# Output projection in four 512-column blocks, and two modulation vectors as TensorE column tiles

## The reference

```python
for i in range(DEPTH):
    mod_lat = silu(c) @ ada_w[i] + ada_b[i]                 # six vectors of 2048
    sh1, sc1, g1, sh2, sc2, g2 = split(mod_lat, 6)
    h_lat = rms_norm(x, norm_mix_g[i]) * (1 + sc1) + sh1
    if i == 0:                                              # 16 heads of 128, 4 key/value heads
        q_l, k_l, v_l = project_qkv(h_lat, ...)             # and rotary on q, k
        k_c, v_c = project_kv(h_ctx, ...)
        o_lat = latent_attention(q_l, k_l, v_l, k_c, v_c) @ attn_w_o
    else:
        o_lat = fourier_mix(h_lat, fourier_w_o)
    x = x + g1 * o_lat
    x = x + g2 * (relu((rms_norm(x, norm_mlp_g[i]) * (1 + sc2) + sh2) @ w1[i]) ** 2 @ w2[i])
return rms_norm(x, final_norm_g)
```

## Time and profile before

| | us |
|---|---|
| median of three runs | 2138.22 (2131.68 to 2138.55) |
| the profiled execution | 2128.54 |
| its span in the trace | 2126.7 |
| TensorE busy | 2018.2 (95%) |
| VectorE busy | 1375.5 (65%) |
| ScalarE busy | 975.3 (46%) |
| mean granted TensorE clock | 0.979 of full |
| mean DMA rate | 253 GB/s |

### The profile page before, as it was taken

How to read it: one execution, slowest core, us unless ns; L and a number is a source line. 1 busy time by engine, 2 the same in 40 slices (tenths; PEclk the granted TensorE clock), 3 DMA queues, 4 the chain that set the end, 5 groups by cost and what they waited for, 6 DMA issues and landing times.

```text
span 2126.7 us, 25114 instructions
## 1 busy us (share of the span) xinstructions
PE 2018.2 (95%) x10348; PEld 1648.6 (78%) x10348; DVE 1375.5 (65%) x1355; ACT 975.3 (46%) x1263; POOL 109.0 (5%) x196
## 2 busy tenths in 40 slices
PE   4999979888999999999999999989999999999997
PEld 3677746656888878788888888878888887888886
DVE  2466879935877868677657866876666545555455
ACT  4433555424445445444444444354554554444443
POOL 1111000100000000000000000000000000000000
PEclk8999999998999999999999999989999999999999
DMA  9798427786998979688759826957777555555653
GB/s 369 280 341 318 168 98 256 260 313 237 335 332 287 358 273 352 241 316 310 268 196 353 349 81 235 377 184 254 246 248 250 188 176 178 198 195 188 213 196 119
DMA packets 140682, 538.89 MB, mean 253 GB/s; under 512 B 8436, under 2 KB 9620, under 8 KB 101012
## 3 DMA queue, kind: packets, MB, share of 16 engines
q1 hardware_dynamic: 106576, 329.73, 44.1%
q0 software_dynamic: 31744, 201.34, 25.8%
q10 hardware_dynamic: 2248, 6.21, 0.8%
HBM read 535.15 MB, written 2.10 MB: 253 GB/s over the span
## 4 chain that ended last, share of the span: by engine, by line
PE 85%; DVE 8%; DMA 3%; ACT 2%; issue 2%; POOL 0%; DVEq 0%; SPq 0%; ACTq 0%; POOLq 0%
PE ps L1515 22%; PE ps L1471 12%; PE ps L1475 12%; PE ps L1474 12%; PE ps L1517 11%; PE ps L1319 4%; PE ps L1320 3%; PE ps L1321 3%; DVE sum_wo L862 1%; DVE ada_sum L862 1%; PE ps L1360 1%; DMA ada_raw<-in_ada_w 1%; DMA c_rows<-in_ctx 1%; DMA spare<-in_ada_w 1%; PE ps L1376 1%
## 5 line engine op out<-in xcount | busy, mean ns | idle before, releaser
L835 DVE TENSOR_TENSOR w_lo<-raw,w_hi 128x1024 fp32r<-128x1024 f32 x624 | 760.1, 1223 | 590.3 <-ACT w_hi L460 590.2
L460 ACT ACTIVATE w_hi<-raw 128x1024 fp32r<-128x1024 f32 x624 | 658.1, 1059 | 905.4 <-PE ps L1475 426.8
L1515 PE MATMUL ps<-hh,w_hi 128*128 128x512 f32 x2048 | 720.0, 397 | 4.0 <-issue 2.6
L1517 PE MATMUL ps<-hh,w_lo 128*128 128x256 f32 x2048 | 571.7, 279 | 0.0
L1515 PEld LDWEIGHTS ps<-hh,w_hi 128*128 128x128 f32 x2048 | 385.4, 188 | 99.7 <-issue 4.2
L1471 PE MATMUL ps<-w_hi,hh 128*128 128x512 f32 x1152 | 449.4, 390 | 6.3 <-DVE u L1258 2.6
L1474 PE MATMUL ps<-w_lo,hh 128*128 128x512 f32 x1152 | 448.8, 390 | 0.0
L1475 PE MATMUL ps<-w_hi,hh 128*128 128x512 f32 x1152 | 448.8, 390 | 0.0
L1517 PEld LDWEIGHTS ps<-hh,w_lo 128*128 128x128 f32 x2048 | 386.6, 189 | 0.0
L1471 PEld LDWEIGHTS ps<-w_hi,hh 128*128 128x128 f32 x1152 | 216.5, 188 | 53.3 <-issue 7.7
L1475 PEld LDWEIGHTS ps<-w_hi,hh 128*128 128x128 f32 x1152 | 216.6, 188 | 45.3
(11 more groups left out here) (191 smaller groups left out, 1361.5 us busy)
## 6 DMA issues: line engine op xcount, KB each, us to landing
raw<-in_mlp_w SPq DMA_DIRECT2D x256, 1024.0 KB, 5.3
ada_raw<-in_ada_w POOLq DMA_DIRECT2D x161, 1024.0 KB, 5.4
raw<-in_attn_w_qkv SPq DMA_DIRECT2D x24, 1024.0 KB, 10.4
spare<-in_ada_w POOLq DMA_DIRECT2D x22, 1024.0 KB, 9.4
raw<-in_attn_w_o SPq DMA_DIRECT2D x16, 1024.0 KB, 5.9
raw<-in_fourier_w_o SPq DMA_DIRECT2D x16, 1024.0 KB, 4.9
g_row<-in_ada_w POOLq DMA_DIRECT2D x9, 1024.0 KB, 10.0
x_tm<-in_x ACTq DMA_DIRECT2D x2, 1024.0 KB, 7.6
```

The lines of the kernel that those rows point to most:

```text
L460: act.activation(w_hi[:, s % SPLIT, :], raw[:, piece % RAW, s % 2, :], ACT.Copy).then_inc(hi_ready, 1)
L835: nc.vector.tensor_tensor(w_lo[:, s % SPLIT, :], raw[:, s // 2 % RAW, s % 2, :], w_hi[:, s % SPLIT, :].bitcast(F32), ALU.subtract).then_in ...
L1515: mm(ps[:, bank, :].rearrange("p (a t) -> p a t", a=2), w_hi[:, s % SPLIT, w], hh[:, k, :, :], start=(k == 0), stop=False, skip_group_chec ...
L1517: ins = mm(ps[:, bank, 0:T], w_lo[:, s % SPLIT, w], h_hi[:, k, :], start=False, stop=(k == KT - 1), skip_group_check=True)
```

## The change

The output projection is cut into four blocks of 512 columns (both token tiles, 96 matmuls each) where it was two halves of 1024. One block is woven into attention, three matmuls a step, and three come behind it. Slices now hold four heads' rows of 512 columns, so that eight slices make a block; the loads are re-laid the same way. The sixteen `ada_step`s of v = 1 leave DVE: v = 1 and v = 2 both become `early_piece`s (four matmuls each in column tiles into bank 2), 24 of them in the attention loop (n = 4, 6, 8, 10, then 12 to 23, then 30 to 37) and 8 in block 1. Their rows of `ada_w` use slots 8, 9, 0, 1 and 10; slot 10 is a new place over the heads 12 to 15 of `hh`, slot 9 one over `q_acc`. Two of v = 0's steps move ahead of attention, so that DVE does step 8 + (p - 18) for each piece p = 18 to 21 of the q, k, v stage. From step 5 on, transposed probabilities alternate between banks 6 and 3. The rows of g1 are turned at n = 33 and 35 within the loop. At the end of the projection the two token tiles are finished one after the other.

```diff
-COLS = {1: 0, 3: 1, 5: 2, 7: 3, 8: 4}
-LAID = {1: 4, 3: 6, 5: 7}
+COLS = {3: 0, 5: 1, 7: 2, 8: 3}
+LAID = {3: 6, 5: 7}
...
+def early_slot(j):
+    if j < 4:
+        return 10
+    return (8, 9, 0, 1, 10)[(j - 4) % 5] if j < 18 else (8, 9, 0, 1)[(j - 18) % 4]
...
+WO_BANKS = (0, 1, 4, 5, 6, 7, 0, 1)
...
+    def turned_bank(m):
+        return 3 if m >= 5 and m % 2 else 6
...
@@ gpsimd, load_vector
-            elif i < 32:
+            elif i < 16:
                 pool.wait_ge(ada_used, i - 1)
...
+            elif i == 16:
+                pool.wait_ge(prod_done, 64)
+            elif i < 20:
+                pool.wait_ge(ada_mm, 16 + i)
+            elif i < 22:
+                pool.wait_ge(head_T, i - 9)
+            elif i < 24:
+                pool.wait_ge(ada_used, i - 7)
+            elif i < 34:
+                pool.wait_ge(ada_mm, i + 12)
             elif i < 48:
-                pool.wait_ge(ada_mm, i - 4)
+                pool.wait_ge(ada_mm, i + 13)
...
+        for j in range(4):
+            load_vector(12 + j)
+            load_vector(16 + j)
...
@@ scalar, attention loop and behind it
-            if n >= 8 and n % 2 == 0:
-                split_hi(52 + (n - 8) // 2)
+            if n >= 10 and n % 4 == 2:
+                split_hi(52 + (n - 10) // 4)
+            if n == 26:
+                rows_early(1)
+            if n == 34:
+                row_out(0, range(2), 4)
+            if n == 36:
+                row_out(0, range(2, 4), 2)
...
-                for k in range(12):
-                    split_hi(first + 16 + k + LOOKAHEAD)
...
+                for i in range(20):
+                    split_hi(60 + i)
+                    if i in (2, 3, 10, 11, 18, 19):
+                        square_banks(0, i // 8 * 2 + i % 2, 1)
+                    if i == 9:
+                        rows_early(2)
@@ vector, q/k/v stage
-            if p in (18, 20):
-                ada_step(0, 8 + (p - 18) // 2)
+            if p >= 18:
+                ada_step(0, 8 + p - 18)
@@ vector, attention loop
-            if n >= 9 and n % 2 == 1:
-                split_lo(52 + (n - 9) // 2)
+            if n >= 11 and n % 4 == 3:
+                split_lo(52 + (n - 11) // 4)
...
-            while taken < 32 and taken - 10 < (n - 3) * 22 // 31 and (taken < 16 or n >= 12):
-                ada_step(taken // 16, taken % 16)
-                taken += 1
-            if n == 30:
+            if n in (3, 5, 7, 9):
+                ada_step(0, 12 + (n - 3) // 2)
+            if n == 14:
                 add_bias(0, g_row)
+            if n == 29:
+                take_early(1)
@@ vector, stage_end
+            if q in BLOCKED:
+                gate_banks(q, 6, 1)
+                total(q, 0)
+                invert(q, 0)
+                for b in range(4):
+                    normed(q, 0, b)
+                gate_banks(q, 7, 1)
+                total(q, 1)
+                invert(q, 1)
+                for b in range(4):
+                    normed(q, 1, b)
...
@@ tensor
+        def early_piece(j):
+
+            slot = vector_slot(16 + j)
+            pe.wait_ge(ada_in[slot], 16 * vector_count(16 + j))
...
+            for b in range(4):
+                ins = mm(ps[32 * b:32 * b + 32, 2, :], silu[:, j % KT, :], ring(slot)[:, 512 * b:512 * (b + 1)], start=(j % KT == 0),
+                         stop=(j % KT == KT - 1), skip_group_check=True)
+            ins.then_inc(ada_mm, 1)
...
+        def block_last(q):
+
+            for k in range(8):
+                for tt in range(2):
+                    block_unit(q, 6 + tt, k)
             for tt in range(2):
...
+                for k in range(8, KT):
+                    block_unit(q, 6 + tt, k)
...
-                wo_half(0, (n - 6) // 2, n % 2)
+                if n % 2 == 0:
+                    pe.wait_ge(o_ready, (n - 6) // 2 + 1)
+                block_unit(0, n % 2, (n - 6) // 2)
+            if n in (4, 6, 8, 10):
+                early_piece((n - 4) // 2)
+            if 12 <= n < 24:
+                early_piece(n - 8)
+            if n == 28:
+                early_cols(1)
+            if n >= 30:
+                early_piece(n - 14)
...
-                if m >= 1:
+                if m >= 5:
+                    pe.wait_ge(probT_out, m - 1)
+                elif m >= 1:
                     pe.wait_ge(probT_out, m)
...
-                for k in range(KT - 2):
-                    for tt in range(2):
-                        wo_half(1, k, tt)
...
+                for b in (1, 2):
+                    for k in range(KT):
+                        for tt in range(2):
+                            block_unit(0, 2 * b + tt, k)
+                        if b == 1 and k % 2 == 1:
+                            early_piece(24 + k // 2)
+                        if b == 2 and k == 4:
+                            early_cols(2)
+                pe.wait_ge(x_blk, 2)
+                block_last(0)
```

More of the change, by code:

```diff
@@ L121, in summed_before, with ops_at, ops_before, full_before @@
 def summed_before(i):
-    return i if i < 32 else i - 16
+    return i if i < 16 else i - 32
+BLOCKED = (0,)
+WO_BANKS = (0, 1, 4, 5, 6, 7, 0, 1)
+def ops_at(q):
+    return tuple((j, 1) for j in range(8)) if q in BLOCKED else ((0, 2), (2, 2), (4, 2), (6, 1), (7, 1))
+def ops_before(q):
+    return sum(len(ops_at(p)) for p in range(q))
+def full_before(q):
+    return sum(4 if p in BLOCKED else 7 for p in range(q))
 V_C, V_CC, V_MIX, V_MLP = 0, 16, 32, 64
@@ L237, in layer_block @@
     raw_in = [sem(f"raw_in{i}") for i in range(RAW)]
-    ada_in = [sem(f"ada_in{i}") for i in range(9)]
+    ada_in = [sem(f"ada_in{i}") for i in range(11)]
     c_in = sem("c_in")
@@ L445, in _ @@
         load_start(31)
-        for i in range(8, 160):
+        for i in range(8, 12):
+            load_vector(i)
+        for j in range(4):
+            load_vector(12 + j)
+            load_vector(16 + j)
+        for i in range(20, 160):
             load_vector(i)
@@ L681, in stage_end @@
         def stage_end(q, next_first):
-            if q:
+            if q not in BLOCKED:
                 square_banks(q, 0, 2)
@@ L1160, in stage_end @@
             gate_banks(q, 7, 1)
-            if middle:
+            if middle and q == 2:
                 middle()
@@ L1178, in stage_end @@
                 normed(q, 0, 3)
+                if middle and q == 1:
+                    middle()
                 invert(q, 1)
@@ L1212, in _ @@
             first = 2 * P_WO[l]
-            v = 2 if l == 0 else 8
+            v = 8
             if l == 0:
-                for k in range(12):
-                    split_lo(first + 16 + k + LOOKAHEAD)
-                    if k in (2, 4):
-                        gate_banks(0, k - 2, 2)
-                    if k == 9:
-                        take_col(1, 1)
+                for i in range(20):
+                    split_lo(60 + i)
+                    if i in (1, 2, 9, 10, 17, 18):
+                        gate_banks(0, i // 8 * 2 + (i - 1) % 2, 1)
+                    if i == 12:
+                        take_early(2)
+                        gain_tm(0, V_MLP, 64, 2)
             else:
```

225 lines of the change are left out of this document (91 added, 134 removed).

## The result

Six times of each kernel gave a median of 2122.16 us after the change (2115.66 to 2125.31) and 2135.69 before it (2131.68 to 2138.55). The ratio of the times is 0.9931, 95% interval 0.9908 to 0.9954, so -14.7 us (-19.6 to -9.8). I had forecast -5 us and 2133. Two later comparisons of the same two kernels gave 0.9957 (0.9943 to 0.9972) and 0.9963 (0.9949 to 0.9978). All 25 times of the changed kernel (three occasions) make 2123.7 in the mean, all 94 of the kernel before (five occasions) 2133.3: -9.6 us. The first six times drew 5 us too much, and the forecast was 4.6 us too small.

The account below looks back on a forecast made before the run. DVE was taken to set the attention loop's pace, TensorE close behind. Terms summed to -6.0 us, a rougher balance gave -4; the middle, -5, made 2123.5 us for the profiled execution or 2133 on the median's scale, range 2122 to 2144.

Parts of the forecast that it names:

- (a): End of the q, k, v stage: a moved DVE step ahead of the last rotary work delays TensorE, +2.3 us.
- (b): Attention steps 0 to 5: an added DVE step and TensorE piece fall into existing waits, 0 us (-1 to +2).
- (c): Attention steps 6 to 13: DVE loses `ada_step`s and splits, 31.5 us against 35.7, -4.2 us (0 to -5.8).
- (d): Attention steps 14 to 31: DVE out of the way, TensorE sets the time, 66.1 us against 72.2, -6.1 (-2 to -7).
- (e) + (f): Steps 32 to 37, +0.4 us; projection behind the loop with more matmuls and single pieces but fewer waits, +4.0 us.
- (g): Last projection matmul to first MLP matmul: first token tile ends earlier, its norm made meanwhile, 8.8 us, -2.4 (-1 to -4).
- (h): Layer 0's last stage: `take_col` moves behind the first tile's norms, 0 us.
- balance of TensorE's work: Step 6 to projection's end: 24.6 us of waits and low clock against 18 us added work; -4 us with (a) and (g).
- rival 4: More gained: steps 6 to 13 pack fully, (a)'s second step hides, no half clock after the loop; -11 us, chance 0.15.
- Rival 2: Loads of `ada_w` rows land late and starve the pieces, holding scores and projection; +8 us, 2146, chance 0.15.
- Rival 3: Loop does not speed up because score to copy passes through three engines; 0 us, 2138, chance 0.15.
- Rival 5: Matmuls get slower with added load streams under them; +7 us if they lose 3% over 230 us, chance 0.05.

## Why the prediction was wrong, point by point

| step | forecast | measured | |
|---|---|---|---|
| (a) end of q, k, v | +2.3 | +2.6 (+3.1 in the first profiles; 2.7 over all) | right in place and cause |
| (b) steps 0 to 5 | 0 | +0.3 (-0.2 to +0.8) | right |
| (c) steps 6 to 13 | -4.2 | -4.1 to -3.5 | right |
| (d) steps 14 to 31 | -6.1 | -7.1 | 1.0 too small, in its last pair |
| (e) + (f) to the projection's end | +4.4 | +4.4 and +2.6 | right; the second profile of before had more low clock |
| (g) to the MLP | -2.4 | -3.0 | 0.6 too small |
| (h) | 0 | 0 | right |
| clock at the MLP's start | no term | -2.1 and -2.3 in two of three, 0 in one | missing |
| sum | -6.0, taken as -5 | -8.9 | |

**Two steps failed: the end of the sum, and a term that stood at nothing.** Of the 3.9 us between -5 and -8.9, 1.0 was lost when I averaged the sum with a rougher one, 1.5 lie in the sizes of the parts up to the MLP, mainly (d) and (g), and 1.4 are the clock at the MLP's start. The mechanism forecast for the loop was right.

The parts gave -6.0, and against the first profiles the same stretches measured -6.9. Then I averaged this with a "balance of TensorE's work" that said -4 and took -5. The balance rested on "2.5 us of waits left over" in a difference of two sums over 20 us each; after the change, TensorE's list shows two waits from 307 us to the end of the loop, 1.1 us together. Here the estimate worked out part by part was the better one, and the middle between the two the worse choice.

**The term that was missing** is the clock at the first MLP matmul. I had put it as a bound of (g) and as part of rival 4. The windows of 4 us, before and then after:

```profile
515.00:519.00 4.00, 4.00 (x13) 3.42 (x14) 3.93 (x6) 1.73 (x4) 0.00 (x0) 0.50 0.80 259
```

```profile
508.00:512.00 4.00, 4.00 (x24) 3.55 (x25) 3.93 (x6) 2.65 (x5) 0.00 (x0) 1.00 0.83 262
```

Clock 0.50 and 13 matmuls before, 1.00 and 24 after. Between the last projection matmul and this one TensorE waited for 6.6 of 11.6 us before, and for 4.9 of 8.6 after. The clock fell in both: after, it is 0.60 from 502 to 506 us, and full again by 508. In the third profile the clock was at a half there again, so this term varies from one execution to the next, 1.4 us in the mean. Over all profiles with the same 8.6 us the first 64 pairs take 24.1 to 24.4 us in six and 25.7 to 26.5 in seven, against 26.4 twice before: 1.2 us in the mean. That the shorter pause makes the full clock likelier fits these counts, but three profiles with the longer pause are too few to show it.

**(d) and (g).** In (d) the pairs with pieces took 8.00 us (forecast 8.0) and those without 5.72 (5.7). With the turn of v = 1 that is 40.0 and 18.0 us, both as summed. The 0.9 us missed are in the last pair: I took 8.0 for steps 30 and 31, and they took 7.07, because step 31 has no score any more (0.85 in my own price). I also compared with 8.0 us a pair for the old loop throughout, which is only its mean. Before, the five pairs from step 13 to 23 took 38.0 us and the four from 23 to 31 34.3; after, 40.0 and 25.1. So the pieces cost 2.0 us where they stand, and the gain of 9.2 lies all behind them. In (g) I had 8.8 against 8.2 measured from the last matmul's end: DVE went on 0.2 us behind that matmul, where I had allowed 0.5 for its norms of the first tile, and the handovers were shorter.

**The rivals.** Rival 2, starved pieces, did not occur: 0.5 us of waiting for a row. It is real all the same, 3.1 us as soon as a row was wanted one step earlier. Rival 3, the chain through three engines, is refuted: steps 24 to 29 take 2.9 us each. Rival 4 was nearest in its figure (-11), and by its clock in two of three profiles, but (a) did not hide as it assumed, and steps 6 to 13 did not pack fully. Rival 5: the matmuls under the load of streams keep their 0.23 us.

**Scale and sample.** I put the forecast on a median of three times, 2138.2; the median of 94 times is 2133.8. That made 2133 where the same difference gives 2128.6. The 2122.16 of the first six times lies just inside my range of 2122 to 2144, with 5 us of it from the draw. And I gave a change within 0.3% the most chance; it was 0.45%.

## What to carry to other kernels

Where an engine of the chain is busy for 95% in a loop, work taken off it returns as time until the next engine is full, and a second buffer beside it may be worth nothing. When parts have been priced from rows, keep their sum; let a rough balance widen the range, not move the value. Price what the clock does behind a pause that the change shortens. Place a moved step where its engine waits for others, not where it has fewest instructions, and let the last block finish one half early.

## What the runs showed of the hardware that I had not expected

- A stream of alternating 512- and 256-column matmuls on full clock runs at one of two paces, 346.7 or 353.3 ns a pair, constant for hundreds of pairs and changed only at an interruption: 5.5 us for one up projection with nothing changed in it, and more than a profile of a small change can bear. Four needless 128x4 matmuls gave the fast pace in three places of three, in one of which all fourteen profiles without them are slow. What decides stays open. The down projection, of 512-column matmuls alone, settles at 43.52 us per 192 matmuls in all sixteen profiles.
- The first full-array matmul behind a column-tile piece takes 0.34 us from start to start, where 0.23 is usual.
- The same kernel's times spread over 13 us (2115.7 to 2129.1 in 25), and the half clock at the first MLP matmul was there in one of three profiles of one and the same kernel. Six times of each kernel gave an interval of -19.6 to -9.8 us where the pooled difference is -9.6.
